# Two layers' rotary turn by transfers within SBUF instead of permutation matmuls, with each head step half a chunk later

## The reference

```
u = h @ w_in
a_b, a_c, a_x, q, k, v, c_in = split(u)
y_a = a_b * short_conv(a_c * a_x)
q, k = apply_rope(q, cos, sin), apply_rope(k, cos, sin)   # per 64-wide half head
a = softmax(q1 k1^T / 8) - lam * softmax(q2 k2^T / 8)      # causal, 4 heads
y_b = rmsnorm(a @ v) * (1 - lam_init)
y_c = silu(layernorm(conv31(glu(c_in))))
x = x + concat(y_a, y_b, y_c) @ w_out ;  x = x + swiglu(rmsnorm(x))

def apply_rope(x, cos, sin):
    x1, x2 = split(x, 2)                    # two halves of 32 of the 64 features
    return concat(x1*cos - x2*sin, x2*cos + x1*sin)
```

## Time and profile before

| | us |
|---|---|
| median of 3 runs (1973.46 to 1976.35) | 1976.17 |
| the profiled execution | 1973.2 |
| its span | 1971.4 |
| TensorE busy | 1910.0 (97%) |
| VectorE busy | 966.4 (49%) |
| ScalarE busy | 737.6 (37%) |
| GpSimd busy | 970.7 (49%) |
| SyncE's DMA queue, share of 16 DMA engines | 25.9% |

### The profile page before, as it was taken

How to read it: one execution, slowest core, us unless ns; L and a number is a source line. 1 busy time by engine, 2 the same in 40 slices (tenths; PEclk the granted TensorE clock), 3 DMA queues, 4 the chain that set the end, 5 groups by cost and what they waited for, 6 DMA issues and landing times.

```text
span 1971.4 us, 28181 instructions
## 1 busy us (share of the span) xinstructions
PE 1910.0 (97%) x8670; PEld 1508.5 (77%) x8670; DVE 966.4 (49%) x1316; ACT 737.6 (37%) x1162; POOL 970.7 (49%) x692
## 2 busy tenths in 40 slices
PE   8999999999999999899999999999899999999996
PEld 6866668888888888567788888888666888888885
DVE  7667654466665224876533333122877443333213
ACT  5245553333232224465433222223455443223222
POOL 4332224446655555843445555554854455555453
PEclk9999999999999999999999999999999999999998
DMA  6211112222222232111222222322111222222332
GB/s 244 65 54 44 45 64 96 96 86 96 96 99 101 98 106 86 65 53 54 86 97 96 96 96 96 101 101 98 64 54 54 75 97 96 96 96 96 100 102 85
DMA packets 48956, 173.94 MB, mean 88 GB/s; under 512 B 5488, under 2 KB 6512, under 8 KB 48624
## 3 DMA queue, kind: packets, MB, share of 16 engines
q1 hardware_dynamic: 48880, 172.96, 25.9%
HBM read 169.82 MB, written 2.10 MB: 87 GB/s over the span
## 4 chain that ended last, share of the span: by engine, by line
PE 81%; DVE 6%; POOLq 3%; issue 3%; DVEq 2%; ACT 2%; POOL 1%; DMA 1%; ACTq 0%; SPq 0%
PE bank L507 21%; PE bank L487 20%; PE bank L488 20%; PE bank L544 3%; PE bank L545 3%; PE bank L551 3%; POOLq L447 3%; PE bank L521 1%; PE bank L527 1%; PE bank L745 1%; DVE lp L1817 1%; PE bank L522 1%; PE bank L774 1%; POOL wl L429 1%; PE bank L788 1%
## 5 line engine op out<-in xcount | busy, mean ns | idle before, releaser
L429 POOL TENSOR_TENSOR wl<-raw,wh (+1 forms) x626 | 883.8, 1433 | 905.6 <-ACT wh L977 892.9
L977 ACT ACTIVATE wh<-raw 128x1024 fp32r (+1 forms) x313 | 331.6, 1060 | 811.9 <-PE bank L507 681.6
L487 PE MATMUL bank<-xh,wh 128*128 128x512 f32 x1336 | 531.3, 398 | 0.7 <-ACT wh L977 0.7
L488 PE MATMUL bank<-xl,wh 128*128 128x512 f32 x1336 | 522.7, 391 | 0.0
L507 PE MATMUL bank<-xh,wl 128*128 128x512 f32 x1336 | 341.5, 395 | 3.5 <-POOL wl L429 3.5
L487 PEld LDWEIGHTS bank<-xh,wh 128*128 128x128 f32 x1336 | 252.5, 189 | 59.5 <-issue 7.1
L507 PEld LDWEIGHTS bank<-xh,wl 128*128 128x128 f32 x1336 | 248.4, 188 | 63.8 <-issue 6.7
L488 PEld LDWEIGHTS bank<-xl,wh 128*128 128x128 f32 x1336 | 252.5, 189 | 56.0 <-issue 3.8
L487 PE MATMUL bank<-hh,wh 128*128 128x512 f32 x528 | 208.0, 394 | 0.0
L488 PE MATMUL bank<-hl,wh 128*128 128x512 f32 x528 | 208.0, 394 | 0.0
L1376 DVE TENSOR_TENSOR ybuf<-bank,rstd 128x512 f32<-128x512 f32 x95 | 65.3, 688 | 224.7 <-PE bank L507 222.7
(11 more groups left out here) (287 smaller groups left out, 2331.9 us busy)
## 6 DMA issues: line engine op xcount, KB each, us to landing
raw<-in_weights SPq DMA_DIRECT2D x313, 512.0 KB, 3.2
xs<-in_x SPq DMA_DIRECT2D x4, 512.0 KB, 6.8
out_t<-xs SPq DMA_DIRECT2D x8, 256.0 KB, 2.1
w1k<-in_w SPq DMA_DIRECT2D x1, 1024.0 KB, 9.5
w1v<-in_w SPq DMA_DIRECT2D x1, 1024.0 KB, 11.2
shifted<-kvraw SPq DMA_DIRECT2D x8, 124.0 KB, 2.4
posi<-in_positions SPq DMA_DIRECT2D x2, 256.0 KB, 8.9
cst<-in_consts SPq DMA_DIRECT2D x1, 290.0 KB, 5.5
```

The source lines that it names most:

```text
L429: x_ = pool.tensor_tensor(wl[:, :, :].rearrange("p s n -> p (s n)")[:, two], raw[:, cols((v % 4) * (CB * P) + h * half, half)], wh[:, :, : ...
L487: mm(b[:, :], w, kh(k), start=first and k == 0, stop=False)
L488: mm(b[:, :], w, kl(k), start=False, stop=False)
L977: return act.activation(o, i, ACT.Copy, scale=scale)
```

## The change

The permutation matmul is gone, with its matrix. SyncE issues four DMAs per tile, each of which copies 32 partitions of `ybuf` to the other half of a group of 64 of a new tile `turned` (two buffers); VectorE multiplies `turned` with the sine. The minus sign of the turn, which was in the matrix, is now in the table of angles. SyncE's loads of chunks 14 to 21 of each layer are taken out of the loop and written out, each behind one tile's four DMAs (`turn_halves`); a tile's DMAs wait for ScalarE's copy and, from the third on, for VectorE's use of the same buffer. ScalarE's copy of tile i waits until the DMAs of tile i - 2 have landed. HEAD_SLOT goes from 21 to 22, so every head step of every engine moves one slot. ScalarE's squares for the layer norm move from slot 40 to 41; the low part of head 3's output, whose step would be slot 44, is written behind the loop. VectorE drains its pipeline ahead of the cosine product. The bank ROT now serves the values only, and `values_l` no longer waits for a sine product to be read.

```diff
@@ -89,7 +89,7 @@
-HEAD_SLOT = 21
+HEAD_SLOT = 22
@@ -282,6 +281,7 @@
+        turned = big("turned", 42, [P, 2, S])
@@ -312,6 +312,7 @@
+        turn_landed = [sem(f"turn_landed{i}") for i in range(2)]
@@ -395,21 +396,45 @@
                             .then_inc(shift_landed, 16)
-            trips = (T_ALL - 8) // 4
-            with sp.Fori(0, trips) as r:
-                for c in range(4):
-                    t = Count(8 + c).loop(r, 4)
-                    chunk, landed, split = t.value(), t.half().value(16), (t + -3).value()
-
-                    for v in (landed, split, chunk * (P * CB * P) * 4):
-                        sp.compute_val(v)
-                    src = weights[bass.ds(chunk, 1), :, :].rearrange("o p c -> (o p) c")
-                    sp.wait_ge(raw_landed[c % 2], landed)
-                    sp.wait_ge(lo_ready, split)
-                    sp.dma_start(raw[:, c * CB * P:(c + 1) * CB * P], src).then_inc(raw_landed[c % 2], 16)
-
-            for t in range(8 + 4 * trips, T_ALL + 2):
-                load(t, t if t < T_ALL else t - T_ALL)
+            def loads(start, end):
+                trips = (end - start) // 4
+                with sp.Fori(0, trips) as r:
+                    for c in range(4):
+                        slot, odd = (start + c) % 4, (start + c) % 2
+                        t = Count(start + c).loop(r, 4)
+                        chunk, landed, split = t.value(), t.half().value(16), (t + -3).value()
+                        for v in (landed, split, chunk * (P * CB * P) * 4):
+                            sp.compute_val(v)
+                        src = weights[bass.ds(chunk, 1), :, :].rearrange("o p c -> (o p) c")
+                        sp.wait_ge(raw_landed[odd], landed)
+                        sp.wait_ge(lo_ready, split)
+                        sp.dma_start(raw[:, slot * CB * P:(slot + 1) * CB * P], src).then_inc(raw_landed[odd], 16)
+                for t in range(start + 4 * trips, end):
+                    load(t, t)
+            def turn_halves(l, i):
+                sp.wait_ge(R["rope_in"], 8 * l + i + 1)
+                if i >= 2:
+                    sp.wait_ge(rot_read, 7 + 8 * l + i - 1)
+                for h in (0, 64):
+                    for a, b in ((h, h + 32), (h + 32, h)):
+                        sp.dma_start(turned[a:a + 32, i % 2, :], ybuf[b:b + 32, i % 2, :]).then_inc(turn_landed[i % 2], 16)
+            done = 8
+            for l in range(LAYERS):
+                T = T_BLOCK1 + l * T_LAYER
+                loads(done, T + 14)
+                for i in range(8):
+                    turn_halves(l, i)
+                    load(T + 14 + i, T + 14 + i)
+                done = T + 22
+            loads(done, T_ALL)
+            for t in range(T_ALL, T_ALL + 2):
+                load(t, t - T_ALL)
 
@@ -869,21 +894,9 @@
 
-                RO = Count(7).loop(l, 8)
                 SS = Count(4 * NU).loop(l, 32)
...
                 SC = (POOLB, TR)
-
-                def rotate_l(i):
-
-                    pe.wait_ge(R["rope_in"], Count(i + 1).loop(l, 8).value())
-                    if i:
-                        pe.wait_ge(rot_read, (RO + i).value())
-                    else:
-                        pe.wait_ge(R["v_out"], Count(NT).loop(l, NT).value())
-                    if i in (5, 7):
-                        pe.wait_ge(sq_ready, Count(8 + (i - 5) // 2).loop(l, 4).value())
-                    mm(ROT[:, :], rot2, ybuf[:, i % 2, :], start=True, stop=True).then_inc(rot_ready, 1)
 
@@ -911,7 +924,6 @@
                     pe.wait_ge(R["pt_ready"], (TT + (4 * h + 4)).value())
-                    pe.wait_ge(rot_read, (RO + min(2 * h + 5, 8)).value())
                     for c in range(NT):
@@ -937,9 +949,6 @@
                         head_step(h, step)
-                    if half == 0 and 9 <= n < 17:
-                        rotate_l(n - 9)
-
                     if s == 38:
@@ -1294,7 +1303,7 @@
                             root(U0 + NORM_LN[0], NT, scale=1.0 / 256, plain=True)
-                        if s == 40:
+                        if s == 41:
                             act.wait_ge(R["ln_sub"], L1.value())
@@ -1303,7 +1312,7 @@
                         if i >= 2:
-                            act.wait_ge(rot_ready, Count(6 + i).loop(l, 8).value())
+                            act.wait_ge(turn_landed[i % 2], Count(64 * (i // 2)).loop(l, 256).value())
                         b = QK0[i] if i < 2 else G[(N + m).even()]
@@ -1769,11 +1778,11 @@
 
-                    dve.wait_ge(rot_ready, Count(8 + i).loop(l, 8).value())
+                    dve.wait_ge(turn_landed[i % 2], Count(64 * (i // 2 + 1)).loop(l, 256).value())
                     if i % 2:
-                        tt(tmp2[:, 0:S], ROT[:, :], sinr, ALU.mult).then_inc(rot_read, 1)
+                        tt(tmp2[:, 0:S], turned[:, i % 2, :], sinr, ALU.mult).then_inc(rot_read, 1)
                     else:
-                        mul3(tmp2[:, 0:S], ROT[:, :], 0.125, sinr).then_inc(rot_read, 1)
+                        mul3(tmp2[:, 0:S], turned[:, i % 2, :], 0.125, sinr).then_inc(rot_read, 1)
                     dve.drain()
@@ -1880,6 +1889,7 @@
                         b = QK0[i] if i < 2 else G[nl_.even()]
+                        dve.drain()
                         dve.wait_ge(R["rope_in"], Count(i + 1).loop(l, 8).value())
@@ -1904,6 +1914,7 @@
                 assert tap[0] >= TAPS
+                y_rest("head3", lo_[:, 1, :])
 
@@ -2048,7 +2057,7 @@
-    consts[:, C["inv2"]] = inv2[p % 32]
+    consts[:, C["inv2"]] = np.where(p < 32, -inv2[p % 32], inv2[p % 32])
...
```

More of the change, by code:

```diff
@@ L68 @@
 _at = 0
-for _name, _n in (("ident", P), ("rot1", P), ("rot2", P), ("ones", P), ("halves", 2), ("inv1", 1), ("inv2", 1),
+for _name, _n in (("ident", P), ("rot1", P), ("ones", P), ("halves", 2), ("inv1", 1), ("inv2", 1),
                   ("rcount", 64)):
@@ L199, in build @@
         rot1 = cst[:, C["rot1"]:C["rot1"] + P]
-        rot2 = cst[:, C["rot2"]:C["rot2"] + P]
         ones = cst[:, C["ones"]:C["ones"] + P]
@@ L2037 @@
     consts[:, C["ident"]:C["ident"] + P] = np.eye(P)
-    for name, dim, half in (("rot1", 16, 8), ("rot2", 64, 32)):
-        for h in (0, 64):
-            for i in range(half):
-                consts[h + half + i, C[name] + h + i] = -1.0
-                consts[h + i, C[name] + h + half + i] = 1.0
+    for h in (0, 64):
+        for i in range(8):
+            consts[h + 8 + i, C["rot1"] + h + i] = -1.0
+            consts[h + i, C["rot1"] + h + 8 + i] = 1.0
     consts[:, C["ones"]:C["ones"] + P] = 1.0
```

## The result

The changed kernel takes 1984.03 us (median, 1981.20 to 1984.38), the one before on the same chip 1976.01 (1973.46 to 1976.35). The ratio is 1.0045, with an interval of 1.0035 to 1.0055: 8 to 9 us slower, where 1.6 us faster was forecast.

A forecast was written before the change was run, and what follows sets the result against it. GpSimd, then a VectorE and ScalarE loop, then TensorE were taken to set the input stage. Per layer +2.1-2.1-0.8 = -0.8 us, -1.6 for two layers, gave 1974.6 us, with a range of 1961 to 1987.

The forecast's parts named there:

- head 1's first score: Input stage: score 4.8 us later, less 2.7 for TensorE standing further on in its stream; loss 2.1 us per layer.
- the two periods: Between first scores of heads 1 to 3: root's wait goes, even turns wait 0.9; gain 0.9 and 1.2, 2.1 us.
- the tail: Head 3's first score to the stage's end: last TensorE wait of 0.91 us nearly gone, 0.8 us gained per layer.
- about three VectorE instructions per half chunk: Late combines change places beside GpSimd, as many meeting it before as after; counted as nothing.
- The permutations alone are worth nothing: TensorE's 16 permutation matmuls, 0.87 us each, 14 us; they count only as far as the VectorE and ScalarE loop shortens.
- The gates on SyncE: Loads ahead of turns 0 to 2 wait for GpSimd's split, opening at 815.28, 823.74 and 829.44 and releasing those turns.
- The turn's length: A tile's four transfers: three issues and a landing, 4.3 us, or 4.65 with a load's own issue ahead.
- rival C: Turns land late, each further us beyond 4.3 costing ten in all; at 5.5 us, 1986.6; chance 0.18.
- low end of 3.2: Shortest length put on a turn, in us, if 32 rows issue in half the time.
- Head 0's first score: Turn 1 lands at 828.4, keys ready at 829.9; TensorE, reaching the score at 827.5, waits 2.4 us.
- The port: Sine products now read two SBUF tiles: 12 in the loop cost 0.9 us more each beside GpSimd, otherwise 0, taken as likelier.
- rival D: Slower through the port: 12 sine products contending with GpSimd add 10.8 us, giving 1985.4; chance 0.12.

The follow-up runs named there:

- psum_noperm: Changed kernel without transfers or permutation matmuls, the sine product reading the idle PSUM bank, swapped halves left out: 0.9996 of the kernel before, 1974.8 us.
- perm22: Kernel before, permutation matmuls kept, with only the head steps moved one slot later (HEAD_SLOT 22): 0.9987 of the kernel before, 1971.5 us.
- The sum's edit: Changed kernel with the sine product written to the idle PSUM bank, where the sum reads it: 0.9976 of the kernel before.
- slot21: Changed kernel with the head steps back at their old slots (HEAD_SLOT 21), transfers kept behind the load: 1.0093 of the kernel before, 1992.7 us.
- turn_first: Changed kernel with each tile's four transfers ahead of the load in SyncE's stream instead of behind it: 1.0022 of the kernel before, 1977.9 us.

## Why the prediction was wrong

The chain of differences that adds up to the result: shift -0.13%, permutations removed +0.09% (psum_noperm against perm22), sine product from SBUF +0.02%, transfers ahead of the load +0.24%, their place behind it +0.23%. Each has an uncertainty of about 0.13%, the two transfer terms stand well out of it.

The prediction's sum had three terms. Measured on the same scale, in us per layer:

| term | forecast | measured |
|---|---|---|
| head 1's first score, less the 2.7 of the shift | +2.1 | +5.7 |
| the two periods behind it | -2.1 | -1.2 |
| the tail | -0.8 | -0.2 |
| sum | -0.8 | +4.3 |

- **The step that failed is the first term, "Loss: 2.1 us per layer".** It counted from turn 2's use, forecast at 82.6 us from the stage's start, and put 15.7 from there to head 1's first score. The use came at 83.2, and from it (835.72) to the score (854.41) 18.7 us passed: 3.0 of the missing 3.6 lie in this path. perm22 has no transfer, and there it takes 18.0 (829.44 to 847.40), so most of it comes with the shift, and the text had it wrong at "about three VectorE instructions per half chunk meet it before and after, so I put nothing for them". The late combines do meet GpSimd in the new order. This is head 0's third combine in the kernel before, 1.1 us in all:

```profile
840.27 0.48 DVE L1817 TENSOR_SCALAR lp<-lp,small 128x384 f32<-128x384 f32 x1
840.83 0.62 DVE L1333 SCALAR_TENSOR_TENSOR lp<-lp,small 128x384 f32<-128x384 f32 x1
```

  and these are the key's sum and the same combine in the changed kernel:

```profile
847.75 1.58 DVE L1787 TENSOR_TENSOR lk<-tmp,tmp 128x512 f32<-128x512 f32 x1
849.49 1.22 DVE L1826 TENSOR_SCALAR lp<-lp,small 128x384 f32<-128x384 f32 x1
850.79 1.49 DVE L1342 SCALAR_TENSOR_TENSOR lp<-lp,small 128x384 f32<-128x384 f32 x1
```

  The sum took 0.9 more than before, this combine 1.6 more, and the first combine with the second peak 3.2 where the text has 2.25; the second combine, put at 0.9 less, took 1.6 less.
- **What the transfers themselves cost was seen in large part.** With the matmul, in perm22, tile 2's use is at 78.4 and not at 83.2. The text had 82.6 and expected the shift to repay it. The shift repaid 0.13% of the time.
- **The permutations alone are worth nothing:** right. Two kernels without them are no faster than perm22.
- **The gates on SyncE:** right in place. Two opened on the forecast's times from the stage's start, one 1.2 us sooner.
- **The turn's length, 4.3 and 4.65 us: too short for the turns that follow a load, too long for the others.** The issues take 2.47 for four, as estimated from the earlier trace rows. The landing took up to 3.9 in place of 2.4 behind a load, 2.0 elsewhere. From the load's issue at 816.38 to the sine product at 822.53 are 6.15 us, not 4.65. That is rival C for three turns of a layer; its price of ten us had the turns late in the periods too, which they are by 0.2 to 0.4 only. The text's low end of 3.2 is a slip: three issues of half the length and the landing are 3.4.
- **Head 0's first score, 2.4 late.** The text counted from turn 1's landing and left turn 0 out, although its own gate, 815.28+4.65, put turn 0 four us behind the time at which its sine product had started in the kernel before:

```profile
815.75 0.68 DVE L1336 SCALAR_TENSOR_TENSOR tmp<-bank,tmp 128x512 f32<-128x512 f32 x1
```

  That product came 5.8 us later from the stage's start. VectorE's stream is in order, so a sum, two taps, a product and a tap were pushed along, and turn 1's product started 1.3 us after the time at which the forecast has it, at 1.75 us in place of 0.7: together the 2.4. The sum of the prediction doesn't use this score; it is reached only through the peak ahead of turn 2's product, which was 0.6 late.
- **The port, "if at none, 0. I take none as likelier": right for the 12 products that it counts,** 0.68 to 0.69 us each, and wrong for the four ahead of them (1.51 to 1.84). By its own rows the price for each would have been 1.0 and not 0.9. The dearer part was not in rival D at all: the sums had two SBUF inputs before too, and the shift took the keys' from 0.77 to 1.58 (1.40 with the transfers). The sum's edit shortens the changed kernel's periods from 21.1, 23.6 and 24.5 to 19.2, 21.5 and 23.3, below the forecast of 19.9, 22.9 and 24.3.
- **The two periods, +2.1 per layer:** the root's wait went as forecast, and the even turns wait 0.35 and 0.40 in place of 0.9. The gain was still 1.2 only; longer key sums and combines stand against it, and how much each takes is not shown.
- **The tail, -0.8:** it is 45.9 against 48.8, but most of that is head 3 starting later in the stream. perm22 has 45.8, so the transfers have no part in the 0.6 that it is longer than forecast; why is open.
- **The reason of shift and transfers together:** slot21 shows that the shift is what makes the transfers bearable. Taken apart, the shift gives 0.13% with permutations and 0.48% with transfers.

What stays open: whether removing the matmuls costs by itself or only within the noise, how the remaining 0.24% of the transfers divides, and why longer tails go with a fallen clock in some layers.

## What to carry to other kernels

Taking a matmul off a busy TensorE is worth nothing where a VectorE loop sets the time, and a DMA in its place can cost: look at what stands ahead of it in the issuing queue and for what that is waiting. When a transfer joins an in-order queue, work out the arrival of the first one, not only of the ones next to the milestone, and follow what it pushes along in the consumer's own stream. When an order changes, don't carry over the lengths that VectorE's instructions had in the old one: see beside whom each will run, those with two SBUF inputs first. Keeping one operand of the sum in PSUM gained 0.45% here, the shift 0.13%, and the transfers lost.

## What the runs showed of the hardware

- A 128x512 product or sum with two SBUF inputs took 0.69 us alone and 1.0 to 1.9 beside GpSimd, and 0.69 throughout, in all 16 sums of a run, once one input lay in PSUM. The Trainium skill (SBUF — State Buffer, Who interferes with whom) says that a VectorE instruction with two SBUF inputs contends with a GpSimd instruction that reads SBUF; the trace agrees, and it weighed 0.45% to 0.77% of this kernel.
- The combine's scaling of a 128x384 tile by a column, with one SBUF tile as input, took 0.48 us where GpSimd was idle and 1.22 beside it: two SBUF tiles are not the only case.
- A transfer of 32 rows (64 KB) within SBUF took 0.59 us to issue on SyncE, hardly less than the 0.64 of the earlier trace rows for twice the rows, and more than a 512 KB load's 0.34. In the changed kernel it landed in 1.9 to 2.4 us when issued 2.6 us or more after such a load's issue, and in 2.4 to 3.9 when issued right behind one.
- TensorE's granted clock fell from 1.00 to 0.50 (2.4 to 1.2 GHz) not only behind the idle 5.8 us but also behind one of 2.68, in psum_noperm, where the first score came at 77.7 and in the other layer, whose clock fell and rose again earlier, at 76.1. A wait of that length doesn't always do it: in turn_first the clock stayed at 1.00 behind one of 2.73 (at 815.47) and fell to 0.54 behind the next, of 2.71. The wait in psum_noperm and the slower matmul behind it:

```profile
824.72 2.86 PE L530 MATMUL bank<-xh,wl 128*128 128x512 f32 x8 [2.68 <-POOL wl L452]
827.38 0.63 PE L510 MATMUL bank<-xh,wh 128*128 128x512 f32 x1
```
